# Four edits inside the mixer of one decoder layer: norm spreads, sample states, softmax scaling, modulation panels

## The reference, cut to what matters

```
qa = l2norm(qa) * 128**-0.5 ; ka = l2norm(ka)            # 8 + 8 heads of 128, after a causal conv
beta = sigmoid(b) ; g = -exp(a_log) * softplus(a + dt_bias)
o_a, s_new = gdn_chunked(...)                            # prompt
S = S*exp(g); delta = beta*(v - k.S); S = S + k delta; o = q.S      # samples: 64 states of 128x128
s = q k / sqrt(128) + mask ; p = exp(s - max) ; p / sum(p) @ v      # attention, per group and head
merged = sigmoid(gate_a)*(o_a @ w_proj_a) + sigmoid(gate_b)*(o_b @ w_proj_b) ; y = merged @ w_out
```

## Time and profile before

| | |
|---|---|
| median of three runs | 2687.14 us |
| the profiled execution: its own time | 2686.34 us |
| its span in the trace | 2684.5 us |
| PE busy | 2628.0 us, 98% |
| DVE, ACT busy | 53%, 39% |
| DMA | 605.58 MB, mean 226 GB/s |

### The profile page before, as it was taken

One profiled execution on the slowest core, in us unless ns is written; L12 is line 12 of the kernel. 1 busy time (PEld: TensorE's weight loads), 2 busy tenths in 40 slices (PEclk: granted clock), 3 DMA queues, 4 the chain that ended last, 5 costly groups with the idle time before them and its releaser, 6 DMA issues.

```text
span 2684.5 us, 49412 instructions
## 1 busy us (share of the span) xinstructions
PE 2628.0 (98%) x21449; PEld 2472.4 (92%) x21449; DVE 1409.7 (53%) x1795; ACT 1053.3 (39%) x1086; POOL 22.5 (1%) x49
## 2 busy tenths in 40 slices
PE   7999999999999999999999999999999999999998
PEld 4889999999999789999989999899899999999997
DVE  3554455444455766655556554375644455444455
ACT  4343333333344433644424444343433333333443
POOL 0000000000000000000010000000000000000000
PEclk9999999999999999999999999999999999999999
DMA  9987755677755887433377565777666655545453
GB/s 398 381 316 265 257 186 191 248 255 264 253 188 187 290 311 274 141 126 111 110 276 266 217 218 206 276 255 270 235 209 232 212 186 191 194 175 185 152 189 129
DMA packets 130576, 605.58 MB, mean 226 GB/s; under 512 B 10464, under 2 KB 10720, under 8 KB 84336
## 3 DMA queue, kind: packets, MB, share of 16 engines
q1 hardware_dynamic: 125584, 582.06, 60.4%
q0 software_dynamic: 4256, 20.59, 2.0%
q10 hardware_dynamic: 576, 0.56, 0.1%
HBM read 590.55 MB, written 12.62 MB: 225 GB/s over the span
## 4 chain that ended last, share of the span: by engine, by line
PE 90%; DVE 4%; DMA 3%; ACT 2%; issue 1%; SPq 0%; DVEq 0%; ACTq 0%; POOLq 0%
PE acc L2101 47%; PE acc L2109 23%; PE acc L2392 4%; PE mp L2190 4%; PE acc L2397 2%; PE acc L2279 2%; DMA raw<-in_ada 2%; DVE wlo L1362 1%; PE mp L2086 1%; ACT whi L889 1%; PE acc L2304 1%; PE mp L2458 1%; PE mp L2463 1%; DMA h<-in_x 0%; PE mp L2168 0%
## 5 line engine op out<-in xcount | busy, mean ns | idle before, releaser
L1362 DVE TENSOR_TENSOR wlo<-raw,whi 128x2048 fp32r<-128x2048 f32 (+2 forms) x427 | 888.7, 2081 | 737.7 <-ACT whi L889 735.2
L889 ACT ACTIVATE whi<-raw 128x2048 fp32r<-128x2048 f32 (+2 forms) x427 | 743.8, 1742 | 495.3 <-PE acc L2109 391.1
L2101 PEld LDWEIGHTS acc<-xhi,whi 128*128 128x128 f32 x3808 | 477.0, 189 | 47.2 <-issue 46.3
L2101 PE MATMUL acc<-xhi,whi 128*128 128x264 f32 x3808 | 509.6, 287 | 1.1 <-ACT whi L889 0.6
L2101 PE MATMUL acc<-xlo,whi 128*128 128x264 f32 x3808 | 499.0, 284 | 0.0
L2109 PE MATMUL acc<-xhi,wlo 128*128 128x264 f32 x3808 | 498.5, 284 | 0.0
L2101 PEld LDWEIGHTS acc<-xlo,whi 128*128 128x128 f32 x3808 | 476.2, 188 | 0.0
L2109 PEld LDWEIGHTS acc<-xhi,wlo 128*128 128x128 f32 x3808 | 475.7, 188 | 0.0
L2109 PE MATMUL acc<-uhi,wlo 128*128 128x264 f32 x1408 | 191.7, 284 | 0.0
L2101 PE MATMUL acc<-uhi,whi 128*128 128x264 f32 x1408 | 190.7, 283 | 0.0
L2101 PE MATMUL acc<-ulo,whi 128*128 128x264 f32 x1408 | 190.1, 283 | 0.0
(11 more groups left out here) (388 smaller groups left out, 1954.2 us busy)
## 6 DMA issues: line engine op xcount, KB each, us to landing
raw<-in_up SPq DMA_DIRECT2D x160, 1024.0 KB, 4.8
raw<-in_ada SPq DMA_DIRECT2D x144, 1024.0 KB, 7.9
raw<-in_down SPq DMA_DIRECT2D x128, 704.0 KB, 4.0
raw<-in_win SPq DMA_DIRECT2D x69, 1024.0 KB, 6.4
raw<-in_wgate SPq DMA_DIRECT2D x32, 1024.0 KB, 4.8
blk<-in_up SPq DMA_DIRECT2D x16, 1024.0 KB, 7.8
raw<-in_wout SPq DMA_DIRECT2D x16, 1024.0 KB, 5.0
raw<-in_wproj SPq DMA_DIRECT2D x24, 512.0 KB, 4.8
```

The source lines that it names most:

```text
L889: act.activation(whi[:, s.slot(SPLIT), 0:width], raw[:, r.slot(RAW), 0:width], ACT.Copy)\
L1362: v.tensor_tensor(wlo[:, s.slot(SPLIT), 0:width], raw[:, r.slot(RAW), 0:width], whi[:, s.slot(SPLIT), 0:width].bitcast(F32), ALU.subtract)\
L2101: mm(dst, whi[:, b, (tile + k) * P:(tile + k + 1) * P], x[part], start=starts and part == 0 and k == 0, stop=False)
```

## The change

1. Spreads go in pairs into the panels: after the first and after the second pass of Z4 to Z7 (`aside`). The gate sums stand with the second pair of Z5. DVE scales heads 0 to 3 behind the gate values, no longer ahead of the low part of Z4.
2. The eight loads of `tbuf` are gone. DVE copies each state panel from `raw` into `tbuf` in halves of 1024 columns (`keep`), and by that frees the raw slot, where PE did so before. The second half of panel 2 is copied only behind `sample_o`.
3. `scale_probs` of both blocks stands ahead of the low part of panel 8 + 2.
4. Modulation panels of attention go in pairs, behind panels 2 and 4, and stand so in the ring.

```diff
+DWA_ADA = (0, 0, 0, 0, 2, 2, 4, 4, 4)
 def r_dwa(p):
-    return At(S_DWA + R2 + (SLOT + 4) * sl + j + min(max(j - 2, 0), 4))
+    return At(S_DWA + R2 + (SLOT + 4) * sl + j + DWA_ADA[j])
...
-                    if 2 <= j < 6:
-                        load_ada(r + 1, G_DWA + sl, j - 2)
+                    if j in (3, 5):
+                        for q in range(2):
+                            load_ada(r + 1 + q, G_DWA + sl, j - 3 + q)
...
-            load_pair(4)
-            load_pair(6)
-            pool.wait_ge(kq_ready, 1)
-            load_pair(0)
-            load_pair(1)
-            pool.wait_ge(wide_folded, 2)
-            load_pair(2)
-            load_pair(3)
-            pool.wait_ge(stored, 16 * 3)
-            load_pair(7)
-            pool.wait_ge(wide_folded, N_STATE)
-            load_pair(5)
...
-                act.wait_ge(slot_done[r.slot(RAW)], (r.turn(RAW) + 1).val())
+                if n < N_STATE:
+                    act.wait_ge(wide_summed, n + 1)
...
-            for c in range(0, 4):
-                l2_scale(c)
             split_lo(At(S_Z + 4), R1)
...
              .then_inc(gates_ready, 1)
+            for c in range(0, 4):
+                l2_scale(c)
...
             split_lo(At(S_GATE + G_LATE + 1), r_gate(G_LATE + 1))
+            def keep(j, half, last):
+                r = At(R_STATE + j)
+                dve.wait_ge(wide_summed, j + 1)
+                ins = v.tensor_copy(tbuf[2 * j + half][:, :, :, :].rearrange("p w h q -> p (w h q)"),
+                                    raw[:, r.slot(RAW), half * PANEL // 2:(half + 1) * PANEL // 2])
+                ins.then_inc(state_kept, 1)
+                if last:
+                    dve.wait_ge(state_kept, last)
+                    dve.sem_inc(slot_done[r.slot(RAW)], 1)
+            keep(0, 0, 0)
+            keep(0, 1, 2)
+            keep(1, 0, 0)
+            keep(1, 1, 4)
+            keep(2, 0, 0)
+            keep(3, 0, 0)
+            dve.wait_ge(stored, 16 * 3)
+            keep(3, 1, 7)
             split_lo(At(S_GATE + G_LATE + 2), r_gate(G_LATE + 2))
...
              .then_inc(sample_o, 1)
+            keep(2, 1, 8)
...
-                    dve.wait_ge(state_loaded[u - 1], 32)
...
-                ahead(SLOT * sl + 2 * G + 1)
                 scale_probs(sl, 0)
                 scale_probs(sl, 1)
+                ahead(SLOT * sl + 2 * G + 1)
...
+            def panel(s, shift, sums, aside=(None, None)):
...
+                        if aside[part]:
+                            aside[part]()
...
             def l2_spreads(first):
-                pe.wait_ge(row_lo, 1)
-                for c in range(first, first + 4):
+                for c in range(first, first + 2):
...
-            l2_spreads(0)
-            full(At(S_Z + 4), R1, At(A_Z + 4), xs)
+            pe.wait_ge(row_lo, 1)
+            full(At(S_Z + 4), R1, At(A_Z + 4), xs, (lambda: l2_spreads(0), lambda: l2_spreads(2)))
...
-            full(At(S_Z + 5), R1, At(A_Z + 5), xs)
-            l2_spreads(8)
...
+            full(At(S_Z + 5), R1, At(A_Z + 5), xs, (lambda: l2_spreads(4), spread_and_sum))
+            full(At(S_Z + 6), R1, At(A_Z + 6), xs, (lambda: l2_spreads(8), lambda: l2_spreads(10)))
+            full(At(S_Z + 7), R1, At(A_Z + 7), xs, (lambda: l2_spreads(12), lambda: l2_spreads(14)))
...
-                wide_sums(r, j, kq[:, j, :, :].rearrange("p w c -> p (w c)")).then_inc(slot_done[r.slot(RAW)], 1)
+                wide_sums(r, j, kq[:, j, :, :].rearrange("p w c -> p (w c)")).then_inc(wide_summed, 1)
...
-                    if 2 <= j < 6:
+                    if j in (2, 4):
...
-                        ada(j - 2, G_DWA + sl, r_dwa(p) + 1)
+                        for q in range(2):
+                            ada(j - 2 + q, G_DWA + sl, r_dwa(p + 1) + 1 + q)
```

More of the change, by code:

```diff
@@ L543, in build @@
         y_stored = sem("y_stored")
-        state_loaded = [sem(f"state_loaded{k}") for k in range(NPAIR // 2)]
+        wide_summed = sem("wide_summed")
+        state_kept = sem("state_kept")
         state_stored = [sem(f"state_stored{k}") for k in range(3)]
@@ L845, in columns @@
                 return x[j // 2][:, j % 2 * 2 * HG * P:(j % 2 + 1) * 2 * HG * P]
-            def load_pair(j):
-                pool.dma_start(tbuf[j][:, :, :, :], columns(t["state"], j)).then_inc(state_loaded[j // 2], 16)
-            load_pair(4)
-            load_pair(6)
-            pool.wait_ge(kq_ready, 1)
-            load_pair(0)
-            load_pair(1)
-            pool.wait_ge(wide_folded, 2)
-            load_pair(2)
-            load_pair(3)
-            pool.wait_ge(stored, 16 * 3)
-            load_pair(7)
-            pool.wait_ge(wide_folded, N_STATE)
-            load_pair(5)
             for j in range(NPAIR):
@@ L894, in wide_copy @@
                 r = At(R_STATE + n) if n < N_STATE else r_cache(n - N_STATE)
-                act.wait_ge(slot_done[r.slot(RAW)], (r.turn(RAW) + 1).val())
+                if n < N_STATE:
+                    act.wait_ge(wide_summed, n + 1)
+                else:
+                    act.wait_ge(slot_done[r.slot(RAW)], (r.turn(RAW) + 1).val())
                 if n >= 2:
@@ L1294, in _ @@
                         act.activation(ahi[:, :, :], oT[:, :, :], ACT.Copy).then_inc(a_hi, 1)
-                copy_rows(G_DWA + sl, r_dwa(SLOT * sl + 5) + 1)
+                copy_rows(G_DWA + sl, r_dwa(SLOT * sl + 5) + 2)
                 take_v(sl, 0)
@@ L2090, in fresh @@
                 pe.wait_ge(acc_taken[a.slot(BANKS)], a.turn(BANKS).val())
-            def panel(s, shift, sums):
+            def panel(s, shift, sums, aside=(None, None)):
                 r = raw_place(s, shift)
@@ L2203, in fold, with full @@
                 last.then_inc(ada_folded, 1)
-            def full(s, shift, a, rows):
+            def full(s, shift, a, rows, aside=(None, None)):
                 fresh(a)
-                panel(s, shift, [(to(a), rows, True, True)])
+                panel(s, shift, [(to(a), rows, True, True)], aside)
             def total_squares(buf, total, n):
@@ L2359, in l2_spreads, with gate_sums, spread_and_sum @@
                     spread(mp[:, 3 * (c % 2), 0:NT], one_l2, ghi, glo, c).then_inc(l2_spread, 1)
+            def gate_sums():
+                pe.wait_ge(tok_ready, 1)
+                pe.wait_ge(masks_loaded, 16)
+                for w, m in enumerate((con[:, C_CUM:C_CUM + P], ones)):
+                    for n in range(NCH):
+                        last = mm(mp[:, 2, (2 * w + n) * H:(2 * w + n + 1) * H], m, tok[:, n, A0:A1],
+                                  start=True, stop=True)
+                last.then_inc(cum_ready, 1)
+            def spread_and_sum():
+                l2_spreads(6)
+                gate_sums()
             full(At(S_Z + 2), R1, At(A_Z + 2), xs)
             full(At(S_Z + 3), R1, At(A_Z + 3), xs)
-            l2_spreads(0)
-            full(At(S_Z + 4), R1, At(A_Z + 4), xs)
+            pe.wait_ge(row_lo, 1)
+            full(At(S_Z + 4), R1, At(A_Z + 4), xs, (lambda: l2_spreads(0), lambda: l2_spreads(2)))
             pe.wait_ge(gates_ready, 1)
@@ L2368, in _ @@
             last.then_inc(gates_turned, 1)
[L2369 to L2376, removed]
-            full(At(S_Z + 5), R1, At(A_Z + 5), xs)
-            l2_spreads(8)
-            full(At(S_Z + 6), R1, At(A_Z + 6), xs)
-            l2_spreads(12)
-            full(At(S_Z + 7), R1, At(A_Z + 7), xs)
+            full(At(S_Z + 5), R1, At(A_Z + 5), xs, (lambda: l2_spreads(4), spread_and_sum))
+            full(At(S_Z + 6), R1, At(A_Z + 6), xs, (lambda: l2_spreads(8), lambda: l2_spreads(10)))
+            full(At(S_Z + 7), R1, At(A_Z + 7), xs, (lambda: l2_spreads(12), lambda: l2_spreads(14)))
             def gate_sixths():
```

## The result

The changed kernel takes 2668.53 us (median of four runs, 2668.22 to 2670.28) against 2687.10 (2686.29 to 2688.66) on the same chip: a ratio of 0.9935, 95% interval 0.9924 to 0.9947. Forecast: 2669.0.

A forecast was written before the change was run, and what follows sets the result against it. PE was taken as the bound, with 90% of the chain of waits. Gains of 5.7 + 6.0 + 3.9 + 2.5 = 18.1 us put the span at 2666.4 and the median at 2669.0, range 2665.5 to 2675.0.

The forecast's parts named there:

- Part 1: Norm spreads, Z4 to Z7: paired spreads between passes cut 34.51 us to 28.8, 5.7 less (bounds 4.0 and 6.3).
- Rival B: Z4 to Z7: the wait moves inside a panel and the clock falls once; gain only 1.9, 2672.8 us; chance 0.05.
- Part 2: Sample states: without pair loads, panel wait and low clock go; 18.33 us become 12.3, 6.0 less (bounds 1.6 and 6.8).
- Part 3: Attention probabilities: earlier scaling saves PE 1.3 us in each of three slices, 3.9 in all (bounds 2.6 and 4.0).
- Part 4: Attention modulation panels in pairs: 0.7 us a slice, less in slice 0; 2.5 in all (bounds 1.5 and 3.0).
- The sum: Whole kernel: 5.7 + 6.0 + 3.9 + 2.5 = 18.1 us off the span, giving 2666.4.
- The lower end of the range: Whole kernel: 2665.5 us, from the upper bounds of Part 1 and Part 2 and 0.5 for the rest.
- Rival D: Any one of the four edits does nothing, the cover being elsewhere: 2671.5 to 2675 us; chance 0.09.
- Rival C: SP's queue: gate panel 28 waits for DVE's eighth copy; PE waits if landing exceeds 9 us; 2693 and above; chance 0.03.

The follow-up runs named there:

- second trace of before: The kernel before, run again unaltered beside the changed kernel on another chip, and traced: 2687.12 us (ten runs), ratio 1.0001.
- the four single kernels: The kernel before with one of the change's four parts each: 2680.55, 2682.22, 2682.82 and 2684.88 us; ratios 0.9978, 0.9986, 0.9987 and 0.9996.

## Why the prediction was right

**Part 1.** Forecast 28.8 us, measured 28.73. The gate values end at 1095.79, 0.6 later than the forecast 1095.2, as DVE's low part began at 1090.64 and not at 1090.1; it waited for ACT's high part. PE came to spread 2 at about 1096.2. Z4's second pass and its pair take 2.76 us (1094.24 to 1097.00), the first 2.42, so the scalings cost 0.34, against 0.3. Rival B is excluded by the same rows; the kernel with the old DVE order shows its mechanism, a wait of 2.8 and a slow pass behind it.

**Part 2.** Forecast 12.3 us, measured 12.09, the wait gone and the clock at its upper level. The copies took 0.69 for one and 1.29 for two, against the 0.9 that I took; the estimate of 0.7 from the Trainium skill, "VectorE: DVE Perf Modes", section on the perf-mode tier table, was the better one, and the trace agrees with it. That changed nothing, since they are hidden. Gate panel 28 went out at 1367.17, about as long before its use as worked out, and did not hold ACT.
What the forecast did not have is that 6.0 us is not a property of the change. The old code's loss behind the wait varies, so the gain for another execution may be half as large or a third larger. That the time came out within 0.5 us is in part luck, since it was reckoned from one trace. Its long spell in the states stood in a trace that reached Z4 early. From the second trace of before the same terms give 2685.2 - (5.7 + 3.1 + 3.9 + 2.5) = 2670.0 for the span, about 2671.9 for the median (an estimate), 3.4 above the measured one though still in the range.

**Part 3.** Forecast 1.3 us three times, measured 2.83 against 4.13 in slice 0 and no wait left in any; alone 4.1 against 3.9.

**Part 4.** Forecast 2.5, measured 3 x 0.73 + 0.16 = 2.35. The term that was mis-sized is slice 0: 0.4 in the sum, 0.16 in the trace. The rows of slice 0 show where 0.6 of the 0.73 stay. The scores start 1454.11 - 1451.80 - 1.94 = 0.37 late, of which 0.22 is the wait for the output norm, which DVE finishes at its own pace, as forecast. And the spreads at 1432.24 now follow a pass and no modulation group, and the first takes 0.2 longer than those at 1447.45, which start at once: PE reaches them before what they wait for is there, or nearly so. DVE's timeline has the low part of those norms end at 1432.19, where PE would have begun at 1432.15. That last reading is from the rows alone and was not tested.

**The sum.** 5.78 + 6.23 + 6.35 = 18.4, less 0.26 of drift elsewhere (+0.51 ahead of Z4, +0.07, -0.32), is 18.1. The lower end of the range does not follow from its terms: 0.6 and 0.8 for parts 1 and 2 and 0.5 for the rest give 2667.1, not 2665.5. The measured time lies inside either. Rival D falls with the four single kernels, of which three are faster beyond their interval and the fourth shows its gain in the trace. Rival C was far off: gate panel 28 had landed when ACT came to it, six us after the issue, and only a copy placed behind the third update brought the queue into play. Its evidence was misread, though: 10.66 was not the longest landing in that stretch, the six gate panels behind it took 14.0 at the median and up to 16.1. At 16.1 and 9 us of room the rival's own sum would have been 7.1 us longer, about 2676.

## What to carry to other kernels

A short wait of PE in a stretch of small products is worth more than its length: price it with the passes behind it, and as a range. Before removing bytes to cure a late load, ask which transfer ran beside it; moving that one in time gave all of the gain. And where old code loses the clock by chance, compare traces stretch by stretch, since medians of single parts need not add up.

## What the runs showed of the hardware

- PE's clock fell to its lower level with PE busy without a gap, in 40 float32 products of 32 columns on end (1361.17 to 1366.6): granted 1.00 from 1362 to 1364, 0.50 from 1366 to 1368. The last wait ahead of them was one of 0.35 us, 19 us earlier.
- The same instructions with waits of 1.34 to 1.64 us at the same panel lost between 3.3 and 7.8 us to wait and clock together, in five traces against 21.15 without the wait.
- A 1 MB load landed in 4.8 us (median of the last two state panels in the changed kernel), where it had taken 10.66 beside loads from POOL's queue, 2 MB asked for just ahead of it and 1.5 MB while it was under way.
- A float32 copy within SBUF of 128x1024 took 0.69 us on DVE, no longer than one of half that width out of PSUM.
